# A two-layer hybrid decoder step: stores and loads moved over stage ends, and three reorderings on VectorE in the mixing stages

## What is computed

```
h = rmsnorm(x)
qkv_a, z, a, b, qkv_b, u, gate_logits = split(h @ w_in)
o_a = gated_deltanet(silu(conv4(qkv_a)), z, a, b)      # 4 heads x 128, chunks
o_b = dilated_window_attention(rope(qkv_b))            # 3 groups x 4 heads x 64
o_c = scale * per_group_map(trailing_mean(u) - u)      # windows 2, 4, 8, 16
x = x + (sum over 3 branches of sigmoid(gate_i) * (o_i @ w_branch_i)) @ w_out
x = x + peer(rmsnorm(x))       # 8 heads, top 16 of 16384 one-neuron experts
```

## Time and profile before

| | us |
|---|---|
| median of 3 runs | 5430.89 |
| lowest and highest | 5428.62, 5431.65 |
| the profiled execution, own time | 5427.78 |
| its span, first to last instruction | 5426.0 |
| mean granted clock of PE | 0.963 of full |

### The profile page before, as it was taken

One profiled execution on the slowest core, in us unless ns is written; L12 is line 12 of the kernel. 1 busy time (PEld: TensorE's weight loads), 2 busy tenths in 40 slices (PEclk: granted clock), 3 DMA queues, 4 the chain that ended last, 5 costly groups with the idle time before them and its releaser, 6 DMA issues. The chain is left out here.

```text
span 5426.0 us, 50085 instructions
## 1 busy us (share of the span) xinstructions
PE 4669.6 (86%) x17274; PEld 2723.6 (50%) x17274; DVE 3005.4 (55%) x7280; ACT 1239.4 (23%) x3097; POOL 1559.2 (29%) x1418
## 2 busy tenths in 40 slices
PE   7899999999898777777788999999999987777776
PEld 5776677755444322232167666777544443323221
DVE  4532323126767799975455233131277677999654
ACT  2221211112222233321122112111122222333211
POOL 0322100003444444444304121000044444444442
PEclk9999999999999999999999999899999999999999
DMA  2223232419999999999812232324299999999997
GB/s 101 78 69 107 73 108 79 145 31 393 416 407 410 421 421 421 421 417 421 348 65 79 80 108 69 104 86 134 90 396 415 405 408 421 421 421 421 417 421 307
DMA packets 338776, 1432.11 MB, mean 264 GB/s; under 512 B 27548, under 2 KB 156438, under 8 KB 190602
## 3 DMA queue, kind: packets, MB, share of 16 engines
q0 software_dynamic: 177376, 1268.07, 57.3%
q1 hardware_dynamic: 158238, 160.40, 9.3%
q10 hardware_dynamic: 2908, 0.43, 0.1%
HBM read 1400.18 MB, written 49.44 MB: 267 GB/s over the span
## 5 line engine op out<-in xcount | busy, mean ns | idle before, releaser
L2655 PE MATMUL ps<-early,diag 128*128 128x512 f32 (+1 forms) x3584 | 1698.9, 622 | 392.1 <-ACT diag L2569 390.5
L2472 POOL DMA_INDIRECT early<-in_peer,ids x896 | 993.2, 1108 | 1811.5 <-PE ps L2655 1238.2
L2655 PEld LDWEIGHTS ps<-early,diag 128*128 128x128 f32 (+1 forms) x3584 | 660.9, 192 | 1388.0 <-issue 726.6
L2497 DVE SCALAR_TENSOR_TENSOR early<-early,rows 128x1024 f32<-128x1024 f32 x896 | 1084.5, 1223 | 460.7 <-DMA early<-in_peer,ids 456.9
L2655 PE MATMUL ps<-late,diag 128*128 128x512 f32 (+1 forms) x1024 | 490.3, 625 | 142.6 <-ACT diag L2569 142.5
L2569 ACT ACTIVATE diag<-consts_sb,weight 128x128 f32<-128x128 f32 (+1 forms) x1152 | 392.9, 388 | 702.1 <-DVE weight L2507 687.9
L1243 PE MATMUL ps<-hT,gate_ring 128*128 128x288 f32 x1536 | 406.6, 420 | 11.5 <-ACT gate_out L1254 9.0
L2561 ACT ACTIVATE gel<-dot 128x2 f32<-128x2 f32 x576 | 117.3, 204 | 1290.3 <-DVE early L2497 980.3
L2655 PEld LDWEIGHTS ps<-late,diag 128*128 128x128 f32 (+1 forms) x1024 | 182.9, 187 | 448.2 <-ACT diag L2569 238.5
L2472 POOL DMA_INDIRECT late<-in_peer,ids x256 | 282.7, 1104 | 343.6 <-PE ps L2655 311.7
L2497 DVE SCALAR_TENSOR_TENSOR late<-late,rows 128x1024 f32<-128x1024 f32 x256 | 309.3, 1222 | 119.5 <-DMA late<-in_peer,ids 119.2
(11 more groups left out here) (368 smaller groups left out, 5563.8 us busy)
## 6 DMA issues: line engine op xcount, KB each, us to landing
gate_ring<-in_w_in POOLq DMA_DIRECT2D x48, 512.0 KB, 4.6
slot<-in_w_branch SPq DMA_DIRECT2D x16, 1152.0 KB, 6.4
ring<-in_w_in SPq DMA_DIRECT2D x8, 2048.0 KB, 9.7
late<-in_peer_query SPq DMA_DIRECT2D x32, 512.0 KB, 18.0
early<-in_peer,ids POOLq DMA_INDIRECT x896
gate_rows<-gate_out POOLq DMA_DIRECT2D x48, 288.0 KB, 2.4
slot<-gate_rows SPq DMA_DIRECT2D x16, 864.0 KB, 8.3
slot<-in_w_in SPq DMA_DIRECT2D x6, 2048.0 KB, 11.4
```

Source lines behind the costliest of these rows:

```text
L2472: pool.indirect_dma_start(place(q), None, table_rows, bass.IndirectOffsetOnAxis(ap=ids[:, n, c:c + 1], axis=0)).then_inc(s.pair[PLACE[q]], 16)
L2497: nc.vector.scalar_tensor_tensor(out=up, in0=up, scalar=1.0, in1=rows[:, n, :], op0=ALU.mult, op1=ALU.mult, accum_out=dot[:, i % 2, k:k + ...
L2655: ins = nc.tensor.matmul(g.ps[0:r, 2 * (n % 2) + m, :], diag[:, q % DIAGS, 0:r], place(q)[:, D + m * 512:D + (m + 1) * 512], start=False, ...
```

## The change

Five things change. (a) In delta_in DVE reads sum c behind the convolution at u = c + 2, one copy earlier than before. (b) In delta_chunks DVE copies the first four of the ten row units; ACT copies the other six. (c) In window_prompt quads and values take banks 5 and 6 in turn, in the order of their events; PE projects gate half 0 ahead of the first quad; ACT takes the exponential of u + 1 behind the first quad copy and gate copy of u; DVE divides unit u (and copies the output of the pair before) ahead of the mask adds of unit u + 1. (d) POOL's last gate store of window_prompt, with the load behind it, is issued at the head of window_samples, and the last store of window_samples at the head of pool_stage. (e) SP's nine stores of pool rows are issued at the head of score_expert_stage, ahead of the load of w_out; DVE waits for them ahead of routing, and ACT ahead of the copies of queries, because those tiles lie where the rows lay. No product, sum or element of a transfer is added or left out.

```diff
@@ delta_in, DVE
-                c = u - 3
+                if 0 < u <= 12:
+                    convolve(u - 1)
+                c = u - 2
                 if 0 <= c < NORMED:
                     dve.wait_ge(s.pe_e, c + 1)
...
-                if 0 < u <= 12:
-                    convolve(u - 1)
@@ delta_chunks
+BY_DVE = 4
+    rows_from = lambda u: (vrow if u % 2 else krow)[0:ROWS[u // 2], u // 2, :]
+    copied = lambda u: (s.rows_copied, u + 1) if u < BY_DVE else (s.act_e, u - BY_DVE + 1)
-                    pe.wait_ge(s.act_e, u - 1)
+                    pe.wait_ge(*copied(u - 2))
-            for u in range(2 * TILES):
+            for u in range(BY_DVE, 2 * TILES):
                 act.wait_ge(s.pe_e, u + 1)
+            for u in range(BY_DVE):
+                dve.wait_ge(s.pe_e, u + 1)
+                nc.vector.tensor_copy(rows_from(u), g.ps[0:ROWS[u // 2], u % 2, :]).then_inc(s.rows_copied, 1)
             dve.wait_ge(s.act_b, 2)
@@ window_prompt
-    quad_bank, value_bank = 5, 6
+    events = []
+    for u, (n, _) in enumerate(units):
+        events += [("quad", u, q) for q in range(-(-len(tiles_of(n)) // 4))] + ([("values", u // 2, 0)] if u % 2 else [])
+    shared_bank = lambda *event: 5 + events.index(event) % 2
+    turns = [event for event in events if event[0] == "quad"]
+    def bank_free(pe, *event):
+        e = events.index(event)
+        if e >= 2 and events[e - 2][0] == "quad":
+            pe.wait_ge(s.act_b, turns.index(events[e - 2]) + 1)
+        elif e >= 2:
+            pe.wait_ge(s.dve_c, events[e - 2][1] + 1)
-            for i in range(len(units)):
+            for i in range(len(units) - 1):
                 gates.store(pool, i)
             def weigh(u):
+                if u == 0:
+                    gates.project(pe, 0)
                 pe.wait_ge(s.dve_b, u + 1)
                 turn(u, 0)
                 if u % 2 == 0 and u + 2 < len(units):
                     scores(u // 2 + 1)
-                gates.project(pe, 2 * u)
+                if u:
+                    gates.project(pe, 2 * u)
@@ window_prompt, ACT
-                if u + 1 < len(units):
-                    exps(u + 1)
+                if u == 0:
+                    gates.copy(act, 0)
...
-                    if q < 2:
-                        gates.copy(act, 2 * u + q)
+                    if q == 0:
+                        if u:
+                            gates.copy(act, 2 * u)
+                        if u + 1 < len(units):
+                            exps(u + 1)
+                    elif q == 1:
+                        gates.copy(act, 2 * u + 1)
@@ window_prompt, DVE
             for u in range(len(units)):
-                if u + 1 < len(units):
-                    first(u + 1)
                 dve.wait_ge(s.act_a, u + 1)
...
                 if u % 2 == 0 and u:
                     last(u // 2 - 1)
+                if u + 1 < len(units):
+                    first(u + 1)
@@ window_samples, POOL
-            for i in range(first_gate // 2, GATE_UNITS):
+            for i in range(first_gate // 2 - 1, GATE_UNITS - 1):
                 gates.store(pool, i)
@@ pool_stage
-            sp.wait_ge(s.act_c, G)
-            sp.dma_start(pool_p[0], new[0:PBUF]).then_inc(s.stored, 16)
-            for b in range(NB):
-                sp.dma_start(pool_s[b, PBUF - NT:], new[PBUF + b * NT:PBUF + (b + 1) * NT]).then_inc(s.stored, 16)
-            sp.wait_ge(s.stored, 16 * (2 + NB))
             clear_other_set(pool, g)
+            gates.store(pool, GATE_UNITS - 1)
+def store_pool(sp, g, o, l, new):
+    sp.dma_start(layer(o["pool_p"], l)[0], new[0:PBUF]).then_inc(g.s.pool_stored, 16)
+    for b in range(NB):
+        sp.dma_start(layer(o["pool_s"], l)[b, PBUF - NT:], new[PBUF + b * NT:PBUF + (b + 1) * NT]).then_inc(g.s.pool_stored, 16)
@@ Output.sync, score_expert_stage
+        store_state(sp)
         sp.dma_start(self.w_out[:], self.w_o).then_inc(s.w_out_in, 16)
+            dve.wait_ge(s.pool_stored, (l + 1) * POOL_STORES)
             for k in range(4):
                 route(0, 0, k)
             out.scalar(act, keys)
+            act.wait_ge(s.pool_stored, (l + 1) * POOL_STORES)
             query(0)
```

More of the change, by code:

```diff
@@ L188, in __init__ @@
         self.gcum = mixing("gcum")
+        self.rows_copied = mixing("rows_copied")
         self.masked = mixing("masked")
@@ L852, in scale_rows @@
                 pool.wait_ge(s.dve_c, n + 1)
-                pool.wait_ge(s.act_e, 2 * n + 2)
+                pool.wait_ge(*copied(2 * n + 1))
                 nc.gpsimd.tensor_tensor(row(kbg, n), row(krow, n), bc(cl[0:r, n, 8:12], 2, HD), ALU.mult).then_inc(s.pool_a, 1)
@@ L1280, in window_stage @@
     next_semaphores(g)
+    return gates
 WB = 384
@@ L1455, in _ @@
         def _(pe):
-            quad = [0]
             def scores(v):
@@ L1499, in values @@
                 pe.wait_ge(s.act_b, quads[2 * v + 1])
-                if v:
-                    pe.wait_ge(s.dve_c, v)
+                bank_free(pe, "values", v, 0)
                 for j, (i, m) in enumerate(tiles):
@@ L1504, in values @@
                         at = i * 256 + (h0 + a) * SD
-                        last = nc.tensor.matmul(g.ps[a * SD:(a + 1) * SD, value_bank, 0:P], vals[:, m, at:at + SD], pT[:, a, j, :],
+                        last = nc.tensor.matmul(g.ps[a * SD:(a + 1) * SD, shared_bank("values", v, 0), 0:P], vals[:, m, at:at + SD], pT[:, a, j, :],
                                                 start=j == 0, stop=j == len(tiles) - 1)
@@ L1564, in last @@
                 dve.wait_ge(s.pe_c, v + 1)
-                nc.vector.tensor_copy(g.ob[:, h0 // 2, cols(n)], g.ps[:, value_bank, 0:P]).then_inc(s.dve_c, 1)
+                nc.vector.tensor_copy(g.ob[:, h0 // 2, cols(n)], g.ps[:, shared_bank("values", v, 0), 0:P]).then_inc(s.dve_c, 1)
             first(0)
@@ L1903, in pool_slab, with pool_stage @@
     return slots[(i + 1) % 2][:].rearrange("p (k c) -> p k c", k=KT)
-def pool_stage(nc, g, t, o, l, oc, slots, merge):
+def pool_stage(nc, g, t, o, l, oc, slots, merge, gates):
     s = g.s
@@ L1915, in pool_stage @@
     smp = lambda i, c: ext[:, i, c, UP:UW].rearrange("p (b j) -> p b j", b=NB)
-    pool_p, pool_s = layer(o["pool_p"], l), layer(o["pool_s"], l)
+    pool_s = layer(o["pool_s"], l)
     G = len(POOLS)
@@ L2411, with score_expert_stage @@
 TURN = [PLACE[:q].count(PLACE[q]) for q in range(PAIRS)]
-def score_expert_stage(nc, g, t, l, rows, sc, sc0, ids, gates, router, late, w_q, out, sb):
+def score_expert_stage(nc, g, t, l, rows, sc, sc0, ids, gates, router, late, w_q, out, sb, store_state):
     s = g.s
@@ L2734, in build @@
             slots = [g.space(AT_LATE + i * SLOT)("slot", [P, SLOT]) for i in range(2)]
-            window_stage(nc, g, t, o, l, slots, slab)
+            gates = window_stage(nc, g, t, o, l, slots, slab)
             oc = g.space(AT_OC)("oc", [P, PW // P, TOK])
             merge = Merge(g, t, l, slots + [g.space(AT_MIX)("slot", [P, SLOT])])
-            pool_stage(nc, g, t, o, l, oc, slots, merge)
+            new = pool_stage(nc, g, t, o, l, oc, slots, merge, gates)
             ffn = g.space(AT_OC)
@@ L2745, in build @@
             out = Output(nc, g, t, l, oc, merge, rows, late)
-            score_expert_stage(nc, g, t, l, rows, sc, sc0, ids, gates, router, late, w_q, out, ffn)
+            score_expert_stage(nc, g, t, l, rows, sc, sc0, ids, gates, router, late, w_q, out, ffn, lambda sp: store_pool(sp, g, o, l, new))
         with ExitStack() as last:
```

22 lines of the change are left out of this document (11 added, 11 removed).

## The result

The kernel after takes 5366.8 us (median; 5366.4 to 5370.3), the kernel before 5431.0 on the same chip. The ratio is 0.9882, with a 95% interval of 0.9871 to 0.9894. The forecast was 5359 with a range of 5346 to 5387: right in sign and range, 71.6 us forecast and 64.3 gained. The profiled execution has a span of 5364.6 (5426.0 before), 61.4 less. A distance to the kernel after is one between medians.

The account below looks back on a forecast made before the run. PE was taken as the bound, busy 86% of the span, so only its waits and slow clock count. Terms of 9.4, 3.3, 7.9 and 15.2 us make 35.8 a layer, 71.6 in all: 5359 us, range 5346 to 5387.

Parts of the forecast that it names:

- A: DeltaNet projections: reading each square sum earlier removes six PE waits of 1.56 us, 9.4 us a layer.
- B: Chunk stage: four row copies by DVE cut PE's wait for ACT, gaining 3.3 us a layer.
- D: Ends of prompt, samples and pool stages: last DMAs moved to the next stage gain 15.2 us a layer, clock included.
- the better of its two bounds: Chunk stage: if the clock stays up, copies pace the transpose groups and the gain is 4.0 us, against 1.9.
- C: Prompt stage: new order of heads gains 15.4 us less 7.5 of added waits, net 7.9 a layer.
- The new waits: Prompt stage: PE's scores for the next pair wait for DVE's mask adds, six times, 7.5 us a layer.
- the 0.8 us of clock gained on the slow turns: Samples stage start: of 2.88 us for twelve slow transposes, about 0.8 is gained, the rest being paced by copies.
- so nothing absorbs it: Expert stages, norms and projections take their time from their own start, so the 71.6 us gain is kept.
- rival (iii): Prompt stage: new waits hold the clock low throughout, making the kernel slower, 5445 us; chance 0.02.
- Rival (i): Prompt stage: the clock falls at the 12 new score waits, 26 us back, 5385 us; chance 0.10.
- Rival (ii): Prompt and samples ends: POOL's landing is not what ends them, 8.3 us a layer lost, 5376 us; chance 0.07.
- Rival (iv): Early starts meet a transfer that is not early, for instance slabs, and time is given back, 5431 us; chance 0.03.

Follow-up runs that it names:

- A: Kernel before with only the order of the delta projection's square sums changed: 5415.9 us against 5430.9, ratio 0.9973.
- A, B: Kernel before with the square sums' order and the row copies on VectorE, without the other parts: 5409.9 us, ratio 0.9964.
- A, B, D: Kernel after with the prompt stage's order of heads, banks and VectorE order as before: 5378.2 us, ratio 0.9906.
- C alone: Kernel before with only the prompt stage's new order of heads and two shared banks: 5421.9 us, ratio 0.9983.
- both undone halves: Two runs on the kernel after: window blocks' last gate stores put back, 5381.8 us; pool state stores issued and awaited at the pool stage's end again, 5380.3 us.
- D alone: Kernel before with only the blocks' last stores (gate rows and pool state) moved into the next block: 5400.7 us, ratio 0.9944.
- the store put back: Kernel after with the last gate store of the prompt and samples blocks issued in its own block again: 5381.8 us.
- B alone: Kernel before with only the first four row copies of the chunk stage on VectorE: 5428.8 us, ratio 0.9998.
- the key copy first: Kernel before with the prompt stage's new order of heads and the samples' key copies put first: 5409.3 us, ratio 0.9961.

## Why the prediction was right, and where it was not

The runs give a chain from before to after, each step beside its term (us, both layers). A step is the difference of two gains, each over the kernel before in its own series; with intervals of 5 to 8 us it shows a size and no more:

| step | forecast | measured |
|---|---|---|
| before to A | 18.8 | 15.0 |
| A to A, B | 6.6 | 3.8 |
| A, B to A, B, D | 30.4 | 31.7 |
| A, B, D to after | 15.8 | 13.7 |

- **A** had the right mechanism: no wait is left and the period is 8.9 (9.1 forecast). With A alone its own stretch gained 17.6 of 18.8 us, and the states and window projection stages gave 4.6 back, 0.6 of it idle time and the rest clock. In the kernel after, A's and B's stretch gained 26.0 (25.4 forecast), and nothing was given back ahead of the prompt stage.
- **B** was right in the chunk stage (3.3 and 3.5 us alone), at full clock as in the better of its two bounds. What it is worth in the whole is not shown: 2 us alone and 3.8 behind A, neither told from zero.
- **C** was right in its own stage. The new waits were forecast at 7.5 us a layer and measured at 7.1. Alone the stage gained 8.4 against 7.9. What was mis-sized is what lies behind the stage: the samples stage took 5.1 us more with C alone. In the full change C is worth 11.4 us by the medians and 13.7 by the table, instead of 15.8.
- **D** was right in size, and its cause is shown by both undone halves. One term was misplaced: the 0.8 us of clock gained on the slow turns. The cover of DVE's clearing and query copies (1.34 and 0.97 us) was that slow clock. With it gone, the turns ran into DVE and PE waited 1.52 us: the thirteenth turn starts 3.48 us behind the stage's start, 3.24 before. And the pool stage, 6.1 and 6.0 us shorter with D alone (6.2 forecast), is 4.7 and 4.3 shorter in the kernel after: its idle time is 3.90 in both, but PE is busy 133.2 and 133.4 us instead of 131.8, at a clock of 0.99 instead of 1.00.
- **The sum** rests on the sentence that the other stages take their time from their own start, "so nothing absorbs it". That step failed: the clock of a stage that is not touched was costed at nothing. In the kernel after the shortfall stands in the samples stage (5.6 and 2.7 us) and the pool stage (1.5 and 1.9). Two slips did no harm: the bounds of A to C add up to 5374 at the slow end, not 5370, and the trace does have a fall that outlasts 7 us of steady work, which rival (iii) says it has not. The kernel before in its samples stage, PE's timeline and the window behind it:
```profile
791.25 6.53 PE L1712 MATMUL ps<-pT,vc 128*128 128x32 f32 x40
...
793.68:803.90 10.22, 10.22 (x39) 8.36 (x39) 1.22 (x4) 0.59 (x1) 0.00 (x0) 0.50 0.14 46
```
PE is busy for all of these 10.22 us, at the lower clock.
- **Rival (i)**, a fall of the clock at the score waits, did not happen: the prompt stage has a clock of 1.00 throughout in layer 1 and, apart from its first 5 us, in layer 2. **Rival (ii)** is refuted by the store put back, and (iii) by the clock of the prompt stage. **Rival (iv)**, gains given back later, came true in part, through the clock and not through a transfer.

The samples stage is the plainest case. Over the runs and layers read here its 821 matmuls took from 119.6 to 131.6 us, with 2.9 to 6.2 us of idle time. Three things can be told apart:

- Before, with A alone, with B alone and with both, it took 126.4 to 126.5 us in all eight layers, although in layer 1 it began at times from 702.7 to 712.9 us. All eight start at the lower clock.
- Behind the same gap of 3.4 to 3.5 us a start at full clock gave 131.6 us, in both layers with C alone and in layer 2 with the gate stores put back; with the key copy first it gave 124.5 in both layers. So the entry bears on the clock far behind it.
- With the gap gone, equal code gave 128.00 and 125.08 us in layer 1.

The Trainium skill ("TensorE: Matmul & The Clock Gate", Part 1) says the clock follows recent activity and is watched at a phase of its own. The spread of the third kind is what this leads one to expect, and the eight equal times show that another start time alone need not change the stage. What sets the later falls stays open: only one profile of each kernel was read, and no run moved the stage's start by a chosen time with all else as it was.

## What to carry over

Ahead of moving work to where it hides, list what was hidden by the slowness that goes: here DVE's 2.3 us of clearing and copies, covered only while PE ran at half clock. When an instruction is put ahead of others in a queue, ask what it waits for itself: the output copy waited 3.3 us for PE with ready mask adds behind it, and swapping the two gave 15 us more. And a gain of a few microseconds in one stage should be checked in the stages behind it, because PE's clock there can move by as much, and in more than one profile, because equal code differed by 1.6 us in one stage and 2.9 in another.

## What the runs showed of the hardware

A stage of unchanged code and nearly unchanged gaps took 5.1 us more (4%) where it began at full clock and PE then waited 0.8 us, in both layers with C alone; with the gate stores put back the two entries stand in one execution, 125.69 and 131.58 us. With that wait gone the stage took 7.1 less. The granted clock was 0.50 over 10.22 us in which PE had no idle time, and it fell within a stretch of forty products 32 columns wide (6.53 us). The states stage, with equal instructions ahead of it, took 50.5 us in five kernels and 52.2 in three. A block did not end before its last DMAs had landed: with a store (2.4 us) or a load (4.5 us) issued at its end PE stood 3.4 to 3.9 us, and 0.7 with them issued in the next block.
